# Attention in pairs: first stages on VectorE together, reciprocals a step later, ScalarE alternating exponentials and copies

## What is computed

```
hn = rmsnorm(h)
proj = hn @ w_in                       # queries, keys, values, gates
o_a  = sliding-window attention, window 128, 8 heads on 2 KV heads, with a sink logit per head
o_b  = g0 * compressed-block attention + g1 * selected-block attention + g2 * window-512 attention
h    = h + (sigmoid(g_a) * (o_a @ w_br_a) + sigmoid(g_b) * (o_b @ w_br_b)) @ w_out
h    = h + mixture of experts (top 2 of 8 in the best of 4 groups) of rmsnorm(h)
out  = rmsnorm(h)
```

## Time and profile before

| what | value |
|---|---|
| median of 3 runs | 1711.31 us (1707.92 to 1711.77) |
| the profiled execution's own time | 1706.61 us |
| its span in the trace | 1704.9 us |
| TensorE matmuls busy | 1566.0 us, 92% of the span |
| VectorE busy | 556.3 us, 33% |
| ScalarE busy | 348.4 us, 20% |
| GpSimd busy | 320.5 us, 19% |
| attention, first scores to the last output copy | 268 to 834 us |

### The profile page before, as it was taken

One profiled execution on the slowest core, in us unless ns is written; L12 is line 12 of the kernel. 1 busy time (PEld: TensorE's weight loads), 2 busy tenths in 40 slices (PEclk: granted clock), 3 DMA queues, 4 the chain that ended last, 5 costly groups with the idle time before them and its releaser, 6 DMA issues.

```text
span 1704.9 us, 21625 instructions
## 1 busy us (share of the span) xinstructions
PE 1566.0 (92%) x7605; PEld 838.1 (49%) x7606; DVE 556.3 (33%) x1538; ACT 348.4 (20%) x859; POOL 320.5 (19%) x466
## 2 busy tenths in 40 slices
PE   6999998898999999899899999689899999999995
PEld 3554543343444444444444455456456666666652
DVE  4210104665656645454322245511011111111115
ACT  3000002443433333333100011111111111111112
POOL 2000002332332323232100111122112212122113
PEclk9999999999999999999999999799999999999998
DMA  9114621443111010100263842579999999999937
GB/s 251 42 41 72 119 79 56 145 170 130 44 25 31 26 44 25 32 25 20 74 229 104 310 164 85 195 281 418 418 421 416 422 357 406 421 418 420 416 140 302
DMA packets 135978, 332.11 MB, mean 195 GB/s; under 512 B 39224, under 2 KB 79576, under 8 KB 126704
## 3 DMA queue, kind: packets, MB, share of 16 engines
q1 hardware_dynamic: 117472, 297.98, 47.7%
q0 software_dynamic: 10048, 21.32, 3.6%
q10 hardware_dynamic: 8400, 12.07, 2.0%
HBM read 276.09 MB, written 55.25 MB: 194 GB/s over the span
## 4 chain that ended last, share of the span: by engine, by line
PE 77%; DMA 8%; DVE 7%; issue 3%; ACT 2%; POOL 2%; SPq 1%; POOLq 0%; ACTq 0%; DVEq 0%
PE PS L809 14%; PE PS L684 11%; PE PS L573 11%; PE PS L823 8%; PE PS L715 6%; PE PS L750 6%; PE PS L631 4%; PE PS L670 4%; DMA WA<-w 4%; PE PS L650 3%; PE PS L568 3%; DMA ids<-ids_d 1%; DVE mx L1109 1%; PE PS L786 1%; PE PS L735 1%
## 5 line engine op out<-in xcount | busy, mean ns | idle before, releaser
L684 PE MATMUL PS<-WA 128*128 128x512 f32 x512 | 259.4, 619 | 17.8 <-ACT WA L917 17.8
L809 PE MATMUL PS<-WA,BA 128*64 128x256 f32 x2048 | 229.5, 381 | 4.5 <-DMA WA<-w 3.5
L809 PEld LDWEIGHTS PS<-WA,BA 128*64 128x64 f32 x2048 | 172.5, 138 | 68.9 <-issue 18.6
L573 PE MATMUL PS<-WA,BA 128*128 128x512 f32 x416 | 181.5, 597 | 4.7 <-DVE WA L1024 4.7
L1359 POOL TENSOR_SCALAR BA<-BA,rin,gates 128x640 f32<-128x640 f32 (+7 forms) x128 | 100.4, 784 | 298.9 <-DVE rin L1132 298.7
L684 PEld LDWEIGHTS PS<-WA 128*128 128x128 f32 x512 | 85.2, 190 | 110.9 <-issue 80.2
L910 ACT ACTIVATE BA<-PS,ngm 128x640 f32<-128x640 f32 (+7 forms) x128 | 89.8, 702 | 216.4 <-DVE ngm L1110 216.2
L1272 DVE SCALAR_TENSOR_TENSOR BA<-BA,PS 128x256 f32<-128x256 f32 x46 | 19.4, 422 | 347.2 <-ACT BA L964 347.2
L573 PEld LDWEIGHTS PS<-WA,BA 128*128 128x128 f32 x416 | 79.1, 192 | 102.4 <-issue 97.1
L823 PE MATMUL PS<-WA,BA 128*64 128x512 f32 x512 | 118.1, 602 | 10.7 <-DVE BA L1282 8.1
L650 PEld LDWEIGHTS PS<-ident,BA 128*128 128x128 f32 x648 | 79.5, 143 | 96.3 <-issue 63.5
(11 more groups left out here) (238 smaller groups left out, 1516.0 us busy)
## 6 DMA issues: line engine op xcount, KB each, us to landing
WA<-w SPq DMA_DIRECT2D x66, 2048.0 KB, 31.0
BA<-w SPq DMA_DIRECT2D x30, 2048.0 KB, 26.6
rows_d<-WA SPq DMA_DIRECT2D x8, 2048.0 KB, 8.3
rows_d<-BA ACTq DMA_DIRECT2D x92, 128.0 KB
WA<-w_in SPq DMA_DIRECT2D x16, 512.0 KB, 5.2
gates_d<-WA SPq DMA_DIRECT2D x32, 256.0 KB, 2.4
WA<-gates_d SPq DMA_DIRECT2D x8, 1024.0 KB, 5.5
BA<-w_in SPq DMA_DIRECT2D x26, 256.0 KB, 5.4
```

The costliest lines, as they stand in the source:

```text
L573: mm = pe.matmul(PS[:, j % 4, :], ws[:, c % 6, k, :], hnT[:, k, 512 * h:512 * h + 512], start=(k == 0), stop=(k == KT - 1))
L684: mm = pe.matmul(PS[:, 6, :], gw[:, j, k, :], hnT[:, k, 512 * hf:512 * hf + 512], start=(k == 0), stop=(k == KT - 1))
L809: mm = pe.matmul(PS[DH * h:DH * h + DH, bank, 0:256], xT[:, k, :], w[par][:, k, 256 * h:256 * h + 256], start=(k == 0), stop=(k == KT - 1))
```

## The change

A `slots` table groups the units in pairs: A units 0 and 1, and 2 and 3; W and S pairs as before; C alone. The loops go over pairs.
- TensorE: both scores of the pair; gate steps of its first unit; values matmuls of the branch that ended two slots before; transposes of the first unit of the slot before; gate steps of the second unit; transposes of the second unit of the slot before.
- VectorE: reciprocal of the second unit of the slot before; first stages of both units; copies for the first unit of the slot before; reciprocal of the first unit of this slot; copies for the second unit of the slot before.
- ScalarE: for the first unit the tanh of a completed gate tile and then the exponential; copies for the first unit of the slot before; exponential of the second unit, then its tanh; copies for the second unit; output copy.
- Scores whose banks were last used by C wait for C's first stage (`front`) instead of its exponential.
- POOL scales both heads of an A unit in one product with a broadcast operand.

```
--- before.py
+++ after.py
@@ -230,6 +230,19 @@
     def unit_cost(u):
 
         return 0.9 + 0.0025 * P * len(u[3]) * (2 if u[1] == "A" else 1)
+
+    slots = []
+    for u, (i, br, h, kbs) in enumerate(units):
+        second = h >= REP if br in "WS" else br == "A" and h % 2 == 1
+        if second:
+            slots[-1].append(u)
+        else:
+            slots.append([u])
+    NS = len(slots)
+
+    def slot(s):
+
+        return slots[s] if 0 <= s < NS else []
 
     NGT = 4 * KT
     ZPARTS = 8
@@ -607,7 +620,12 @@
             k0 = P * kbs[0]
             pair = br in "WS"
             if u >= 2:
-                pe.wait_ge(S["exp_done"], u if pair else u - 1)
+                freed = u if pair else u - 1
+                if units[freed - 1][1] == "C":
+                    pe.wait_ge(S["exp_done"], freed - 1)
+                    pe.wait_ge(S["front"], freed)
+                else:
+                    pe.wait_ge(S["exp_done"], freed)
             if u == 0:
                 pe.wait_ge(S["proj_act"], len(jobs) // 2)
                 pe.wait_ge(S["proj_dve"], len(jobs) // 2)
@@ -686,16 +704,23 @@
             if k == KT - 1:
                 mm.then_inc(S["gate_in"], 1)
 
-        for n in range(NU + 3):
-            if n < NU:
-                if units[n][1] in "AC" or units[n][2] < REP:
-                    scores(n)
-                for step in steps_at[n]:
+        for s in range(NS + 2):
+            for u in slot(s):
+                if units[u][1] in "AC" or units[u][2] < REP:
+                    scores(u)
+            for u in slot(s)[0:1]:
+                for step in steps_at[u]:
                     gate_step(step)
-            if 2 <= n < NU + 2:
-                turn(n - 2)
-            if n >= 3 and (n - 3) == last_of[units[n - 3][:2]]:
-                values(*units[n - 3][:2])
+            for u in slot(s - 2)[-1:]:
+                if u == last_of[units[u][:2]]:
+                    values(*units[u][:2])
+            for u in slot(s - 1)[0:1]:
+                turn(u)
+            for u in slot(s)[1:2]:
+                for step in steps_at[u]:
+                    gate_step(step)
+            for u in slot(s - 1)[1:2]:
+                turn(u)
 
 
         for dt in range(KT):
@@ -888,46 +913,63 @@
             last.then_inc(S["evac_act"], 1)
 
 
-        for n in range(NU + 3):
-            if n < NU:
...
-                last.then_inc(S["exp_done"], 1)
-                for m in tile_done_at.get(n, ()):
-                    act.wait_ge(S["gate_in"], m + 1)
...
-            if 2 <= n < NU + 2:
-                for m in range(first_group[n - 2], first_group[n - 1]):
-                    if m % 2 == 0:
-                        move_group(m)
-            if n >= 3 and (n - 3) == last_of[units[n - 3][:2]]:
...
+        def exponential(n):
+
+            i, br, h, kbs = units[n]
+            act.wait_ge(S["front"], n + 1)
+            if n >= 3:
+                act.wait_ge(S["t_done"], first_group[n - 2])
+            nk = P * len(kbs)
+            s0, v = 2 * (n % 2), n % 4
+            if br == "A":
+                nc.scalar.activation(esk[:, v, :], esk[:, v, :], ACT.Exp)
+                for g in range(2):
+                    last = nc.scalar.activation(PB[:, n % 3, nk * g:nk * g + nk], PS[:, s0 + g, 0:nk],
+                                                ACT.Exp, bias=ngm[:, v, g:g + 1], scale=SC,
+                                                accum_out=den[:, v, g:g + 1])
+            elif br == "C":
+                last = nc.scalar.activation(pc[:, :, :], pc[:, :, :], ACT.Exp, scale=SC)
+            else:
+                src = PS[:, s0:s0 + 2, :].rearrange("p a n -> p (a n)")[:, 0:nk]
+                last = nc.scalar.activation(PB[:, n % 3, 0:nk], src, ACT.Exp, bias=ngm[:, v, 0:1], scale=SC,
+                                            accum_out=den[:, v, 0:1])
+            last.then_inc(S["exp_done"], 1)
+
+        def gate_tiles(n):
+
+            for m in tile_done_at.get(n, ()):
+                act.wait_ge(S["gate_in"], m + 1)
+                if m >= 2:
+                    act.wait_ge(S[f"gst{m % 2}"], 16 * (m // 2))
+                nc.scalar.activation(gst[:, m % 2, :], PS[:, 6, :], ACT.Tanh, scale=0.5).then_inc(S["gate_act"], 1)
+
+        def move_groups(u):
+
+            for m in range(first_group[u], first_group[u + 1]):
+                if m % 2 == 0:
+                    move_group(m)
+
+        def move_output(i, br):
+
+            act.wait_ge(S["pv_done"], pv_order.index((i, br)) + 1)
+            act.wait_ge(S["s_ready"], last_of[(i, br)] + 1)
+            dst = (qa if br == "A" else qb)[:, :, P * i:P * i + P]
+            nc.scalar.copy(dst, PS[:, 7, :].rearrange("p (r t) -> p r t", r=REP)).then_inc(S["o_evac"], 1)
+
+        for s in range(NS + 2):
+            for u in slot(s)[0:1]:
+                gate_tiles(u)
+                exponential(u)
+            for u in slot(s - 1)[0:1]:
+                move_groups(u)
+            for u in slot(s)[1:2]:
+                exponential(u)
+                gate_tiles(u)
+            for u in slot(s - 1)[1:2]:
+                move_groups(u)
+            for u in slot(s - 2)[-1:]:
+                if u == last_of[units[u][:2]] and units[u][1] in "AS":
+                    move_output(*units[u][:2])
 
 
         act.wait_ge(S["merge_ps"], 2 * KT)
@@ -1132,19 +1174,27 @@
                 dve.reciprocal(rin[:, v, 0:1], den[:, v, 0:1]).then_inc(S["back"], 1)
 
 
-        for n in range(NU + 2):
-            if n < NU:
-                front(n)
-            if 1 <= n < NU + 1:
-                back(n - 1)
-            if n >= 2:
-                for m in range(first_group[n - 2], first_group[n - 1]):
-                    if m % 2 == 1:
-                        dve.wait_ge(S["t_done"], m + 1)
-                        slot_free(dve, m)
-                        for dst, src in group_copies(m):
-                            last = dve.tensor_copy(dst, src)
-                        last.then_inc(S["evac_dve"], 1)
+        def take_groups(u):
+
+            for m in range(first_group[u], first_group[u + 1]):
+                if m % 2 == 1:
+                    dve.wait_ge(S["t_done"], m + 1)
+                    slot_free(dve, m)
+                    for dst, src in group_copies(m):
+                        last = dve.tensor_copy(dst, src)
+                    last.then_inc(S["evac_dve"], 1)
+
+        for s in range(NS + 1):
+            for u in slot(s - 1)[1:2]:
+                back(u)
+            for u in slot(s):
+                front(u)
+            for u in slot(s - 1)[0:1]:
+                take_groups(u)
+            for u in slot(s)[0:1]:
+                back(u)
+            for u in slot(s - 1)[1:2]:
+                take_groups(u)
 
 
         for pi in range(2 * KT):
@@ -1348,9 +1398,8 @@
             nk, v = P * len(kbs), n % 4
             pool.wait_ge(S["back"], n + 1)
             if br == "A":
-                for gg in range(2):
-                    pr = PB[:, n % 3, nk * gg:nk * gg + nk]
-                    last = g.tensor_scalar(pr, pr, rin[:, v, gg:gg + 1], None, ALU.mult)
+                pr = PB[:, n % 3, 0:2 * nk].rearrange("p (g k) -> p g k", g=2)
+                last = g.tensor_tensor(pr, pr, rin[:, v, 0:2].unsqueeze(2).to_broadcast([P, 2, nk]), ALU.mult)
             elif br == "C":
                 last = g.tensor_tensor(pc[:, :, :], pc[:, :, :], rin[:, v, :].unsqueeze(2).to_broadcast([P, 8, 64]), ALU.mult)
             else:
```

More of the change, by code:

```diff
@@ L888, in move_group @@
             last.then_inc(S["evac_act"], 1)
-        for n in range(NU + 3):
-            if n < NU:
[L893 to L911, removed]
-                last.then_inc(S["exp_done"], 1)
-                for m in tile_done_at.get(n, ()):
-                    act.wait_ge(S["gate_in"], m + 1)
-                    if m >= 2:
-                        act.wait_ge(S[f"gst{m % 2}"], 16 * (m // 2))
-                    nc.scalar.activation(gst[:, m % 2, :], PS[:, 6, :], ACT.Tanh, scale=0.5).then_inc(S["gate_act"], 1)
-            if 2 <= n < NU + 2:
-                for m in range(first_group[n - 2], first_group[n - 1]):
-                    if m % 2 == 0:
-                        move_group(m)
-            if n >= 3 and (n - 3) == last_of[units[n - 3][:2]]:
-                i, br = units[n - 3][:2]
-                if br in "AS":
-                    act.wait_ge(S["pv_done"], pv_order.index((i, br)) + 1)
-                    act.wait_ge(S["s_ready"], last_of[(i, br)] + 1)
-                    dst = (qa if br == "A" else qb)[:, :, P * i:P * i + P]
-                    nc.scalar.copy(dst, PS[:, 7, :].rearrange("p (r t) -> p r t", r=REP)) \
-                        .then_inc(S["o_evac"], 1)
```

## The result

The changed kernel takes 1666.01 us, median of 4 runs (1665.36 to 1668.36), against 1709.66 us of the kernel before (4 runs, 1707.92 to 1711.77). The ratio is 0.9749, 95% interval 0.9737 to 0.976: 2.5% or about 43 us faster. The forecast was 1674.7 us, range 1661 to 1695. The profiled execution of the changed kernel took 1666.44 us, with a span of 1664.6 us against 1704.9, so 40 us of the difference stand in the two traces.

What follows compares the result with a forecast made beforehand. TensorE, busy 507 of attention's 566 us, was taken as the bound, with about 59 us idle to win. Gains of 13.8, 8.9, 7.2, 5.7 and 1.0 sum to 36.6 us: median 1674.7 us, range 1661 to 1695.

Steps and rivals of the forecast that it cites:

- The ledger and its window: List of what ended TensorE's idle time in attention, 268 to 834 us: 59 us is nearly all the change can win.
- Tanh ahead of the exponential: ScalarE's queue, first unit of a pair: gate matmuls' 17.8 us of waits for the tanh fall to 4, gain 13.8 us.
- The rival of the held exponential: On ScalarE the tanh waits for TensorE and holds the exponential behind it: 16 us come back, 1690.7 us, chance 0.15.
- Both first stages together: VectorE's copy leaves the scores' chain: of 23.9 us waiting for exponentials and final copies 15 stay, gain 8.9 us.
- The pair formulas: Scores-to-scores chain times per pair: 6.1 us for five blocks with few gate steps, 7.06 for eight blocks without.
- the slower rival: Block rows 4 to 7: transposes wait for VectorE's copy behind the second first stage, 1729 us at worst, chance 0.05.
- Scores behind C: Scores after the compressed branch wait only for VectorE's subtraction, not the exponential: 8.7 us of waits fall to 1.5, gain 7.2.
- POOL: Transposes waiting for POOL's scaling: one product of 1.04 us and an earlier reciprocal cut 7.2 us to 1.5, gain 5.7.
- The sentence on the reciprocal: Remark in the POOL term that VectorE's reciprocal of u-1 comes before the first stages instead of between; no separate size.
- At nothing: the place of the values matmuls: TensorE does values matmuls before instead of after the transposes of u-2: same work, costed at nothing.
- The clock: TensorE's lower-clock stretches in attention cost about 1.1 us each; fewer waits may save one or two, gain 1.0 us.
- The four classes: TensorE's waits for tanh, exponentials with final copies, branch C and POOL: gains 13.8, 8.9, 7.2 and 5.7 us.

## Why the prediction was right, point by point

**The ledger and its window.** Right. The time came from attention and from nowhere else, most of it from TensorE's idle time there.

**Tanh ahead of the exponential.** Right, gain 16.2 us of waits where 13.8 were taken. I left 4 us and 1.6 stayed. Alone on the old kernel it is worth 12 to 13 us, undone on the new one 10. The rival of the held exponential did not appear: all waits of scores for exponentials are 5.5 us, where it wanted 16 to come back.

**Both first stages together.** What is left was right: 15 us against 15.0 measured. That is not one lucky total: block rows 0 and 1 have 2.6 us for 3, rows 2 and 3 2.6 for 1.5, rows 4 and 5 2.2 for 2.3, row 6 1.6 for 2, and row 7 with the drain 6.1 for 6.2. The 8.9 us are no price of this part, though. Undoing it costs 40 us, or 24 with the values matmuls behind, and alone on the old kernel it gives 4. The pair formulas held too: 6.07 us measured against 6.1, and for the pair of eight blocks without gate steps 6.98 us (766.18 to 773.16) against 7.06. The wait for VectorE's copies was named and is there, 4.0 us in 5 places, so the slower rival had the right place, and 4 of the 54 us of its worst price. One price in it was wrong: it gives 0.8 us of waiting for a pair with two gate steps, but by its own figures the copy is done at 5.3 us and TensorE comes to the transposes at 4.57 less 0.76, which makes 1.5; 1.59 were measured.

**Scores behind C.** The mechanism was right, the term was mis-sized: "I leave 1.5 of 8.7" became 4.0. I let the transposes of the A pair cover the wait everywhere but in block rows 0 and 4. All eight rows have it, 0.4 to 1.0 us each. For VectorE takes up C's first stage only behind the copy for A and the reciprocal of the last A unit, and the copy waits for TensorE's transposes as well (4.33 us idle before it in block row 4). The run with the old condition has 8.6 us, so that cover was worth nothing and the condition 4.6.

**POOL.** The total of the waits was right (1.1 left, 1.5 said), the duration too. The cause was wrong in part. Splitting the product again costs no time that the runs can tell, while putting one reciprocal behind C's first stage costs 21 us in the new loops. The sentence on the reciprocal carried the part, and the product's 0.8 us lies under another wait.

**At nothing: the place of the values matmuls.** It is worth some 3 us at most (3.6 us of waits, times not clear of noise), and the copies' place decides whether it is free: with a copy between the first stages it costs 14.

**The clock.** I took 1.0 us. The low stretch of the earlier trace rows is gone, but the last pairs lose more clock than before (0.82 and 0.66, against 0.83 and 0.83), so the term came to nothing, 5.1 us missing before and 5.2 after. The Trainium skill's page "TensorE: Matmul & The Clock Gate", Part 1, says that the throttled state is the default and activity releases it; by that the last pairs should recover once their idle time goes. The run with gate steps in all units agrees, with 1.00 in both windows.

**The size.** 36.6 us were predicted and 40.9 are the stage's difference in the traces. The four classes gave 35.9 us (16.2 + 8.9 + 4.7 + 6.1) where the sum has 35.6. That this is so close is in part luck: the tanh gave 2.4 us more and C 2.5 less. The whole idle time fell by 34.2, since small waits outside the classes grew. The other 6.7 us are busy time, where the sum had 1.0 for the clock and nothing else, and their cause stays open. The signs of the prediction show the same: it looked for 23 us idle in a stage of 530 us, and found 25 in one of 525.6.

The forecast of the median, 1674.7 us, came out 8.7 too high. 3.6 of that is this difference (1670.0 against 1666.44 for the profiled execution). 4.7 is the step from the profiled execution to the median, which the kernel before had (1706.61 against 1711.31) and the changed one has not (1666.44 against 1666.01).

What the prediction did not say, and the runs did, is that the ledger adds up for the change as a whole only. VectorE's order alone gives 4 us, the tanh alone 13, and the whole 43; undone one at a time the parts cost 40, 21, 19, 10, 4, 3 and 1 us, a sum of 98 (the last three not clear of noise).

## What to carry to other kernels

A ledger of what ended the bottleneck engine's idle time, with a chain worked out for one pair of each size, gave each class of waits to within 3 us. It does not price the parts one by one: a step in one queue is free only as long as another queue's order keeps it free. Here a copy of some 0.6 us in front of the second first stage of 46 pairs cost 24 us over the whole stage, and 40 us once its input stood behind long matmuls. When a stage ends, look at whether filler work is left for its last steps, since idle time there can also cost clock.

## What the hardware showed

Nothing contradicted what was expected of single instructions. The two-input product with a broadcast on POOL took 1.04 us for 512 columns in the A units as in C. The one thing larger than expected was the price of a wait near the end: 2.75 us idle twice, and eight matmuls that then took 3.61 us where 1.99 is usual (the kernel before has a batch of 3.01 us there).
